# A decoder block with 32 experts: h added in place, 1 MB of down weights loaded earlier, the final gain broadcast by TensorE

## The reference

```
h = concat(meta, x);  u = rms_norm(h, g_mix);  z = u @ w_in            # 1024 -> 2048
c_val, c_gate, r_x, r_gate = split(z, 4)
mix = concat(conformer_conv_group(c_val, c_gate, ...), griffin_group(r_x, r_gate, ...))
h = h + mix @ w_out
u = rms_norm(h, g_ffn)
logits = u @ w_router + b_router;  vals, idx = top_k(logits, 4);  wts = softmax(vals)
for each expert e of 32:                  # g = its gate per token, zero where not chosen
    hgu = u @ w_gate_up[e] + b_gate_up[e]                              # 1024 -> 2048
    x_glu = min(hgu[:, 0::2], 7);  x_lin = clip(hgu[:, 1::2], -7, 7)
    act = x_glu * sigmoid(1.702 * x_glu) * (x_lin + 1)
    acc += g * (act @ w_down[e] + b_down[e])                           # 1024 -> 1024
h = rms_norm(h + acc, g_final);  return h[meta tokens dropped]
```

## Time and profile before

| | us |
|---|---|
| runs: median (lowest to highest of 3) | 1034.5 (1033.51 to 1035.92) |
| the profiled execution | 1034.31 |
| its span | 1032.4 |
| TensorE (PE) busy | 985.7, 95% |
| VectorE (DVE) busy | 247.8, 24% |
| ScalarE (ACT) busy | 141.2, 14% |
| moved by DMA | 419.63 MB, 406 GB/s over the span |

### The profile page before, as it was taken

One profiled execution on the slowest core, in us unless ns is written; L12 is line 12 of the kernel. 1 busy time (PEld: TensorE's weight loads), 2 busy tenths in 40 slices (PEclk: granted clock), 3 DMA queues, 4 the chain that ended last, 5 costly groups with the idle time before them and its releaser, 6 DMA issues.

```text
span 1032.4 us, 11631 instructions
## 1 busy us (share of the span) xinstructions
PE 985.7 (95%) x4760; PEld 394.9 (38%) x4760; DVE 247.8 (24%) x661; ACT 141.2 (14%) x259; POOL 24.8 (2%) x15
## 2 busy tenths in 40 slices
PE   9999999999999999999999999999999999999996
PEld 7888533333333332333333332333333333333332
DVE  6997411111111111011111110111111120111122
ACT  3235311111011110011100100111111100011112
POOL 0260000000000000000000000000000000000000
PEclk9999999999999999999999999999999998999999
DMA  8996799999999999999999999999999999999995
GB/s 245 322 405 262 278 404 427 428 427 433 430 430 427 427 432 434 433 429 430 432 430 425 431 431 437 429 376 429 430 431 435 427 434 429 430 428 428 429 424 210
DMA packets 44288, 419.63 MB, mean 406 GB/s; under 512 B 5980, under 2 KB 22508, under 8 KB 24805
## 3 DMA queue, kind: packets, MB, share of 16 engines
q1 hardware_dynamic: 43524, 418.90, 97.1%
q10 hardware_dynamic: 736, 0.34, 0.1%
HBM read 418.18 MB, written 1.05 MB: 406 GB/s over the span
## 4 chain that ended last, share of the span: by engine, by line
PE 65%; DMA 29%; DVE 2%; ACT 2%; issue 1%; SPq 0%; DVEq 0%; ACTq 0%
DMA dn_ring<-in_w_down 29%; PE bank L1239 27%; PE bank L1271 18%; PE bank L1078 6%; PE bank L1220 4%; PE bank L1195 3%; PE bank L1186 2%; PE bank L1099 1%; ACT reg L605 1%; PE bank L1256 1%; PE bank L1250 1%; PE bank L1034 0%; PE bank L1313 0%; DVE gu_ring L806 0%; PE bank L1151 0%
## 5 line engine op out<-in xcount | busy, mean ns | idle before, releaser
L1239 PE MATMUL bank<-gu_ring,reg 128*64 128x512 f32 x2048 | 447.3, 594 | 0.9 <-DVE reg L898 0.9
L1239 PEld LDWEIGHTS bank<-gu_ring,reg 128*64 128x64 f32 x2048 | 144.2, 137 | 301.0 <-issue 298.2
L1271 PE MATMUL bank<-dn_ring,reg 128*64 128x512 f32 x768 | 172.6, 596 | 25.5 <-DMA dn_ring<-in_w_down 20.9
L932 DVE TENSOR_SCALAR reg<-bank 128x256 f32<-128x256 f32 x64 | 24.2, 419 | 646.9 <-PE bank L1239 646.9
L1271 PEld LDWEIGHTS bank<-dn_ring,reg 128*64 128x64 f32 x768 | 53.7, 137 | 132.9 <-issue 99.9
L600 ACT ACTIVATE reg<-reg 128x512 f32<-128x512 f32 x30 | 18.9, 629 | 463.7 <-DVE reg L932 463.7
L1220 PE MATMUL bank<-reg 64*128 64x512 f32 x256 | 63.6, 615 | 1.0 <-DVE reg L981 0.9
L1271 PE MATMUL bank<-dn_odd,reg 128*64 128x512 f32 x256 | 58.5, 598 | 3.8 <-ACT reg L605 3.8
L1195 PE MATMUL bank<-xh,reg 128*64 128x512 f32 x256 | 60.4, 592 | 0.0
L1078 PE MATMUL bank<-reg,gu_ring 128*128 128x272 f32 (+1 forms) x256 | 58.5, 390 | 0.8 <-DVE reg L720 0.8
L1078 PEld LDWEIGHTS bank<-reg,gu_ring 128*128 128x128 f32 x256 | 48.5, 190 | 9.9 <-issue 0.9
(11 more groups left out here) (216 smaller groups left out, 436.1 us busy)
## 6 DMA issues: line engine op xcount, KB each, us to landing
gu_ring<-in_w_gate_up SPq DMA_DIRECT2D x48, 4096.0 KB, 31.9
dn_ring<-in_w_down SPq DMA_DIRECT2D x40, 2048.0 KB, 25.3
gu_ring<-in_w_gate_up SPq DMA_DIRECT2D x32, 2048.0 KB, 19.4
dn_odd<-in_w_down SPq DMA_DIRECT2D x16, 2048.0 KB, 29.3
dn_ring<-in_w_down SPq DMA_DIRECT2D x16, 1024.0 KB, 11.7
gu_ring<-in_w_in SPq DMA_DIRECT2D x16, 512.0 KB, 7.3
dn_ring<-in_w_out SPq DMA_DIRECT2D x4, 1024.0 KB, 8.3
xh<-in_x SPq DMA_DIRECT2D x2, 512.0 KB, 4.1
```

The lines of the kernel that those rows point to most:

```text
L932: ins = V.tensor_scalar(half(xglu, b), glu_v[:, 0], 7.0, None, ALU.min)
L1239: ins = mm(gub[b][64 * h:64 * h + 64, :], xgT[:, j, :], gu_ring[:, s, j, 1024 * h + 512 * b:1024 * h + 512 * b + 512], start=False, stop=( ...
L1271: ins = mm(db[64 * h:64 * h + 64, :], actT[:, at:at + SLOTS], w[:, k, 512 * h:512 * h + 512], start=(k == 0), stop=(k == KD - 1))
```

## The change

- `hT` is now `xT[:, :, META:]`: VectorE adds the output projection in place over the raw x. `reg2` is free once the input projection has read `uT`.
- The first 1 MB of expert 1's tail is loaded into `reg2[:, 0:2048]` (`dn_1`), behind `second_load(3)`. The down product of expert 1 takes steps 4 and 5 from there (`moved=True`). Its old issue, ahead of `y_ps >= 1`, is gone; the second 1 MB stays where it was.
- `g_final` is loaded as two rows of 512 into `tails` (4 KB) in the trunk. Behind `list_tables` the new `gain_rows` makes two products of 128x512, a column of the identity held over 128 columns against the two rows, and waits for `gfin_ok`: VectorE copies both from PSUM to `gfin` behind `q_ok`.
- `LIST` goes from 12 to 7: the list, `add_b_down` and `gain_rows` lie in and behind experts 14 and 15.

```diff
-LIST = 12
+LIST = 7
...
-        hT = reg2[:, 0:KD * SEQ].rearrange("p (d t) -> p d t", d=KD)
+        hT = xT[:, :, META:]
+        dn_1 = reg2[:, 0:2 * D].rearrange("p (k n) -> p k n", k=2)
...
+        gfin_rows = tails[NE:NE + 2, :]
...
+            sp.dma_start(gfin_rows, g_final.rearrange("(b n) -> b n", b=2)).then_inc(gfin_in, 16)
...
             second_load(3)
+            sp.dma_start(reg2[:, 0:2 * D], quarter_rows(1, 0)).then_inc(dn_1_in, 16)
             sp.wait_ge(wout_used, 2)
...
             second_load(1)
-            sp.wait_ge(back_ps, 4)
-            sp.dma_start(gfin, g_final.partition_broadcast(P)).then_inc(gfin_in, 16)
 
             gu_quarters(1, 2, (1, 2, 3, 4))
-            tail_quarters(1, 0)
+            sp.wait_ge(y_ps, 1)
+            sp.dma_start(quarter_slot(1), quarter_rows(1, 1)).then_inc(tail_q[1], 16)
             head(2, 0, 0)
...
-                V.tensor_tensor(hT[:, d, :], hacc(d), xT[:, d, META:], ALU.add).then_inc(h_ok, 1)
+                V.tensor_tensor(hT[:, d, :], hacc(d), hT[:, d, :], ALU.add).then_inc(h_ok, 1)
...
             v.wait_ge(q_ok, 1)
+            v.wait_ge(gfin_ps, 1)
+            V.tensor_copy(gfin[:, 0:512], db[:, :])
+            V.tensor_copy(gfin[:, 512:1024], tb[:, :]).then_inc(gfin_ok, 1)
...
-            v.wait_ge(gfin_in, 16)
+            v.wait_ge(gfin_ok, 1)
...
-                    if quarters and k in (4, 6):
-                        pe.wait_ge(tail_q[k // 2 - 2], tails * 16)
+                    if moved and k == 4:
+                        pe.wait_ge(dn_1_in, 16)
+                    elif quarters and k in (4, 6):
+                        pe.wait_ge(tail_q[k // 2 - 2], (tails - (k == 4 and n > 1)) * 16)
...
-                    w = dn_odd if odd and k < 4 else dn_ring
+                    w = dn_1[:, k - 4, :] if moved and k in (4, 5) else (dn_odd if odd and k < 4 else dn_ring)[:, k, :]
...
+            def gain_rows():
+
+                pe.wait_ge(gfin_in, 16)
+                for b, out in ((0, db), (1, tb)):
+                    ins = mm(out[:, :], ident[NE:NE + 2, NE + b:NE + b + 1].to_broadcast([2, P]), gfin_rows, start=True, stop=True)
+                ins.then_inc(gfin_ps, 1)
+                pe.wait_ge(gfin_ok, 1)
...
             list_tables()
+            gain_rows()
             add_b_down()
```

More of the change, by code:

```diff
@@ L238, in build @@
         tail_q = [sem("tail_q0"), sem("tail_q1")]
+        dn_1_in, gfin_ps, gfin_ok = sem("dn_1_in"), sem("gfin_ps"), sem("gfin_ok")
         gu_used = [sem("gu_used0"), sem("gu_used1")]
@@ L1257, in act_turned, with down @@
                 ins.then_inc(aT_ps, 1)
-            def down(n, odd, heads, tails, quarters=False):
+            def down(n, odd, heads, tails, quarters=False, moved=False):
                 pe.wait_ge(aT_ok, n + 1)
@@ L1263, in down @@
                         pe.wait_ge(head_in[odd], heads * 16)
-                    if quarters and k in (4, 6):
-                        pe.wait_ge(tail_q[k // 2 - 2], tails * 16)
+                    if moved and k == 4:
+                        pe.wait_ge(dn_1_in, 16)
+                    elif quarters and k in (4, 6):
+                        pe.wait_ge(tail_q[k // 2 - 2], (tails - (k == 4 and n > 1)) * 16)
                     if not quarters and k == 4:
                         pe.wait_ge(half_in, tails * 16)
-                    w = dn_odd if odd and k < 4 else dn_ring
+                    w = dn_1[:, k - 4, :] if moved and k in (4, 5) else (dn_odd if odd and k < 4 else dn_ring)[:, k, :]
                     at = (k % 4) * P + (k // 4) * SLOTS
                     for h in range(2):
-                        ins = mm(db[64 * h:64 * h + 64, :], actT[:, at:at + SLOTS], w[:, k, 512 * h:512 * h + 512],
+                        ins = mm(db[64 * h:64 * h + 64, :], actT[:, at:at + SLOTS], w[:, 512 * h:512 * h + 512],
                                  start=(k == 0), stop=(k == KD - 1))
@@ L1288, in expert_up, with expert @@
                     before_down()
-            def expert(n, s, loads, before, heads, tails, quarters=False, **extra):
+            def expert(n, s, loads, before, heads, tails, quarters=False, moved=False, **extra):
                 expert_up(n, s, loads, before, **extra)
-                down(n, 1 - s, heads, tails, quarters)
+                down(n, 1 - s, heads, tails, quarters, moved=moved)
             def list_places():
@@ L1348, in _ @@
             expert(0, 1, 1, None, 1, 1, quarters=True, freed=PK)
-            expert(1, 0, 1, 0, 1, 2, quarters=True, freed=PK)
+            expert(1, 0, 1, 0, 1, 2, quarters=True, freed=PK, moved=True)
             expert(2, 1, 2, 1, 2, 3, quarters=True, freed=PK)
```

## The result

| | before | after |
|---|---|---|
| median of 12 runs (lowest to highest), us | 1034.65 (1033.24 to 1037.08) | 1037.34 (1036.14 to 1039.48) |
| ratio, 95% interval | | 1.0025 [1.0017, 1.0032] |
| profiled execution, span | 1034.31, 1032.4 | 1036.87, 1034.9 |

The kernel became slower by 2.6 us (by the ratio), clear of noise. The forecast was 1033.7 us, and its range ended at 1036.8.

What follows compares the result with a forecast made beforehand. Weight transfers bound the kernel up to expert 19's end, then TensorE. The turn's +0.2 and the end's -0.85 gave -0.6 us, so 1033.7 us from the profiled 1034.31; the range was 1030.9 to 1036.8.

Steps and rivals of the forecast that it cites:

- the turn: At y(19), where SyncE's queue order changes and the DMA engines run dry; forecast 0.2 us later than before.
- waits for gate/up halves: TensorE's waits from about expert 25 on, forecast to replace all but 0.85 of the list's 10.6 us.
- T: Extra time over TensorE's pace in expert 16, from the list's surplus of 8.1 plus the new wait: 10.5 us.
- y(15): Moment expert 15 is done: forecast 569.06 us; the weights would allow 568.6, so no wait is left.
- the new wait: Behind the list: two g_final products (0.96), VectorE's two copies (1.4) and two hand-overs, 2.45 us in all.
- The clock inside T: Lower clock level behind the list's narrow products, 6.8 us as before, putting 3.4 us into T.
- the middle one: The case in which the clock at the list falls as before, with T=10.5 us.
- y(14): Moment expert 14 is done: forecast 539.44 us, 2.4 earlier through the early 1 MB.
- y(19): Moment expert 19 is done: forecast 688.0 us, where the weights would allow 685.4.
- The end: Behind expert 29's second gate/up half, landing at 950.2 us, TensorE finishes at 969.35: 0.85 us gained.
- In-place h, the old broadcast and the 4 KB load at 0: VectorE's in-place additions, g_final's removed 0.5 MB broadcast and its replacement load in the trunk: each taken as 0 us.
- Rival 2: From the wait for VectorE's copies into expert 16, the clock stays low: T=13.9, 1037.1 us, slower; chance 0.15.

Runs made afterwards that it cites:

- e4: The changed kernel with LIST=5, the list at experts 10 and 11: ratio 0.9977 to the kernel before.
- e8: The changed kernel with LIST=6, the list at experts 12 and 13: ratio 0.9988 to the kernel before.
- e11: The changed kernel with LIST=5, without the g_final products and their wait, the broadcast issued behind the last down weights: ratio 0.9981 to the kernel before.
- e12: e11 with expert 21's first gate/up half issued ahead of expert 20's second down half: 1030.28 us, ratio 0.9962 to the kernel before.
- e10: The changed kernel (LIST=7) without the g_final products and their wait, the broadcast issued behind the last down weights: ratio 0.9978 to the kernel before.
- e1: The changed kernel with LIST back at 12, the early 1 MB and g_final products kept: ratio 1.0031 to the kernel before.
- e6: The changed kernel with the two g_final rows in partitions 32 and 64 instead of 32 and 33: ratio 1.0012 to the kernel before.
- e9: The changed kernel run once more, unaltered: ratio 1.0026 to the kernel before.
- e5: The changed kernel with LIST=12, no g_final products or wait, the broadcast issued behind the last down weights: ratio 0.9979 to the kernel before.
- e3: The changed kernel with TensorE's wait for gfin_ok moved behind the four b_down products: ratio 0.9995 to the kernel before.
- e7: The changed kernel with unused products into a free bank filling TensorE's three stalls at the list's end: ratio 1.0027 to the kernel before.
- e2: The kernel before with LIST=7 alone, g_final still by broadcast and no early 1 MB: ratio 1.0001 to the kernel before.

## Why the prediction was wrong

The mechanism was right and is shown: TensorE's lateness at the list is free until the turn (e4, e8, e11), there it dries the queue up (41 GB/s, e12), and what the list no longer costs at experts 24 to 26 turns into waits for gate/up halves (the chain's 801.40 34.14). Wrong was the size of terms in T and in y(15), against a margin at the turn that the prediction had itself put at 0.2 us.

- **The term that failed: the new wait, "2.45 us", in T.** It measured 4.51 in the profile after, and 4.50 by taking it out (e10). Nearly all of the difference is the two products: 3.07 us instead of 0.96. It has two parts. First, the four records were priced with the eight of line 1220 in 1.92 us, 0.24 each. But those are pairs that read different halves of the partitions, so they lie in different row groups and run beside each other, and the two products lie in one row group. At full clock their four records took 1.99 us (e1), twice as long each. e6 shows that the row group is the cause: put into two of them, the four took 1.71 instead of 3.07 us. That is 1.0 us of the error. Second, the other 1.1 us is the low clock over them. It was in the text as a condition ("If the clock is at half, the products cost 1.0 more") and was left out of the sum.
- **The clock inside T.** Three cases were named and the middle one, 6.8 us, was taken; it was 10.2, and 13.7 in e9. The price of the longer fall is small where it lies over VectorE's copies: in the profile after, b_down, bias and gate/up took 3.78, 1.91 and 14.29 us, 3.1 over their times at full clock (1.99 in e5, 1.02 and 13.88 in the earlier trace rows); before it was 3.2.
- **y(14).** The early 1 MB was taken at 2.4, and that was right. The first half of expert 2's down matrix landed at 149.39+10.0 = 159.4, 2.0 ahead of 161.4, in an execution whose y(0) was 0.5 later. Counted from y(0), y(14) is 2.3 ahead of before, and y(19) is 2.3 and 2.4 ahead in e1 and e5. So of the 0.6 us by which y(14) missed, 0.5 is the trunk of this one execution. (The estimate of 3.6 us for this gain, on which nothing rests, should read 3.7: 161.4-157.7.)
- **y(15).** The weights were to allow 568.6 plus TensorE's 0.5. Instead the second half of expert 15's down matrix landed 26.9 us after its issue, not 25.3 as the five before it, and TensorE still had to wait for it (the piece 540.01 26.88). 1.1 us, in no term. All runs with the list ahead of the turn have a late landing at the list's second expert, e4, e11 and e12 at expert 11; e1 and e5 don't. So the experts that waited for down weights were 9 to 15, not 8 to 14.
- **Sum.** y(19) was to be 688.0 and was 691.60: 0.6 (y(14)), 1.1 (y(15)), 1.9 (expert 16: 39.55 against 37.62). The 27.10 of the others held.
- **The end** was to give back 0.85; it gave 1.3: turn +3.8, span +2.5. The slack was read at the second gate/up half of expert 29, where the chain did not end. At the head of the last down matrix, where it ended, the landing was 3.6 us later (1017.50 against 970.57+43.3 = 1013.9), and TensorE in the profile before took it up only 1.2 us after its landing (`1015.05 3.65 PE L1271 MATMUL bank<-dn_odd,reg 128*64 128x512 f32 x16`); 3.6 less 1.2 is the 2.5 of the span within 0.1. Nor did the stream keep the turn's shift, as the prediction had it: the half of expert 29 landed 2.2 us later (914.54+37.86 = 952.4 against 950.2), not 3.8. The landings in the trace say where the 1.5 us went: one at 745.7 us in the profile before came 11.3 us behind the one ahead of it instead of 9.7, and all behind it stayed as late; the changed kernel has no such step there, but a smaller one at 982.8 us.
- **In-place h, the old broadcast and the 4 KB load at 0:** nothing in the profile after speaks against it; e5 and e10, which have the in-place h, are ahead of before, and in e1, e3, e4 and e8, which load the two rows in the trunk, y(0) is 148.1 to 148.8 against 148.52.

Rival 2, "the new wait keeps the clock low", with a chance of 0.15, named the side and came within 0.3 us of both the time (1037.1 against 1037.34) and the turn (691.4 against 691.6). Much of that is luck: it needed T=13.9, and T was 12.45; the missing 1.5 us came from y(15) and the later trunk, which it did not have. A T of its size does occur: 41.24-27.10 = 14.1 in e9. Its cause is not shown: with the wait moved behind b_down (e3) the clock was low for the same 10.2 us, and with the stalls filled (e7) for 13.7 us in the profile, though some of e7's other runs speak for it. The term that failed could have been closed by asking what the eight records of line 1220 run beside.

## What to carry to other kernels

A stage that waits for weights absorbs work only as far as the next place where the queue depends on the engine: count its waits up to there (here four of 2.1 us) against the whole of what is moved. If that comes out even, move it earlier or take it out; a forecast with a margin of 0.2 us can fall to either side. When a profile is to decide between causes, look at where its time stands among the other runs of the same kernel: e7's was the slowest of 11. Price a single product by a single product: a mean per record taken from pairs that run in different row groups halves it. And a dry spot of a queue at a change of order is time for everybody behind it; one transfer issued earlier there (e12) was worth 2.0 us by the ratios, about as much as the 1 MB at the front.

## What the runs showed of the hardware that was not expected

- The granted clock fell at the list in 13 of 14 profiles, always 0.3 to 2.8 us behind the last of the narrow products of the tables, and for 3.4, 6.8, 10.2 or 13.7 us; in e5 it did not fall, with the same instructions there as before. It was shortest without the g_final products (3.4 to 6.8, or none; six profiles) and 10.2 or more with them (eight). What decides the length stays open. The Trainium skill (TensorE: Matmul & The Clock Gate, HAM oscillation — how this bites in real kernels) lays the fall to gaps in which TensorE is idle; the profile of e7 does not agree, for TensorE is busy 9.93 of 10 us there and the clock falls all the same.
- Products in different row groups run beside each other even when they belong to different lines: in e3 b_down vanishes between the g_final products, at 0.04 us per pair of records.
- The late landing at y(15): the landings in the trace show one of the 16 DMA engines completing its share of that half 1.2 us behind the next to last (566.9 against 565.7 us; 0.6 before, 567.2 against 566.6), at constant GB/s. An instruction fetch of 16 KB, which takes 1.1 us, runs at 562.5 us there; before, none runs between 313 and 739 us. The step of the profile before at 745.7 us also follows such a fetch, at 740.0, that of the profile after at 982.8 one at 980.6, and e1 and e5 have one at 821 us behind a fetch at 819. Behind the step at 745.7 the 16 engines finish each transfer 2.5 us apart instead of 1.0, up to 979 us and beyond. Not every fetch has a step behind it (none at 594.9 us in the profile after), and no run moves a fetch alone, so that it is the cause is not shown.
- In four of the profiles (e2, e7, e9, e11) the clock dropped for 3.4 us in the trunk's first 16 us, and y(0) was 1.2 to 1.8 us later than before.
